# Hybrid decoder step: key steps ahead of the attention units, the block chain spread over them, query tiles upwards, value steps in the last eight units

## The chip, the core and the metric

One Trainium2 chip, one of its cores. The metric is the device time of one launch in microseconds (us), the median of several runs. The core has five engines that run their own instruction streams and meet at semaphores: PE (TensorE, matrix products into eight PSUM banks), DVE (VectorE), ACT (ScalarE), POOL (GpSimd) and SP (SyncE). SP, ACT and POOL start DMAs; sixteen DMA engines carry them.

## What is computed

One inference step of a one-layer decoder, for a prompt of 512 tokens and for 8 samples of 8 new tokens with 2048 past tokens each, all in float32. Cut to what matters:

```python
q, kv_cmp, kv_slc, kv_win, gates, u = in_projection(x, ...)           # one product with w_in
kc, vc = compress_blocks(kv_cmp, cmp_pos_emb, w_cmp_k, w_cmp_v, ...)  # 64 tokens of a block -> 1 key, 1 value
#   kc = einsum('bnlkd,lde->bnke', blk[..., 0], w_cmp_k), then RMSNorm;  vc likewise, without the norm
o_cmp, p_kv = compressed_attention(q, q_pos, kc, vc, slopes)
idx, valid  = select_blocks(p_kv, q_pos, nb)                          # top 16 blocks of 64 tokens
o_slc = selected_branch(q, q_pos, kv_slc, idx, valid, slopes)
o_win = window_attention(q, q_pos, kv_win, k_pos, slopes)             # last 512 tokens
A = gates0 * o_cmp + gates1 * o_slc + gates2 * o_win
h = x + concat(A, pool_mix(u)) @ w_out
y = h + hier_moe(rmsnorm(h))                                          # 16 experts, 2 for each token
```

For the samples the past tokens of the compressed and of the selected branch lie in pages of 128 tokens in HBM and are found through a page table: 16 pages for each of 8 samples.

## The kernel before, in words

The kernel is one hand-ordered program. Each engine has one block of code, and the order in it is the order of its instructions; a semaphore for each PSUM bank says that it is filled or read (`opened`, `filled`, `written`, `read`, `taken`), and `psum_plan` walks the same loops to give every named product its bank. In order of time:

1. Input projection (to about 127 us), PE at work all the time.
2. Pooling mixer in four groups, then the transposes of the queries and keys of five row tiles.
3. Prompt attention, here called **the units**. A unit u is one entry of `prompt_pairs()`: query tile i (128 queries), head pair g, branch b (selected or window). There are 32. Tile i attends to i + 1 blocks of 128 keys, so a unit of tile 3 costs four times the columns of a unit of tile 0. `AHEAD` = 3: in the pass of unit u of the loop PE makes the scores of unit u + 3 (L1047), then transposes the exponentials of unit u (L1091), and in every second unit multiplies with the values (L1060). DVE turns the scores into logits (L1886) and copies one half of the transposes back (L1938), ACT takes the exponentials (L1506) and copies the other half (L1535). PE's transposes of unit u + 1 need DVE's and ACT's copies of unit u. After four units the shares are multiplied in (L1071, L1906 to L1912).
4. Sample attention in four pairs of samples (`s_scores`, `s_values`), first line L1113.
5. Output projection, router, and the experts (from about 490 us), where PE is at work nearly all the time.

**Block compression** runs beside stages 2 and 3 in two rounds of HD = 64 steps: round 0 for keys, round 1 for values. A step d is four small products on PE (L914, eight records in a trace) and needs chunk d of the cached rows, regrouped for it. POOL regroups all chunks of round 0 (L2319); in round 1 POOL does every second, DVE (L1945) and ACT (L1556) every fourth. The chunks lie in a ring of `RING` = 13: chunk d may be written when step d - 13 is done. The key steps are spread: `AT_HEAD` before the mixer, `AT_MIX` in each of its groups, `AT_TURN` behind each row tile's transposes, the rest in the units of `CMP_UNITS`; the value steps are all in units.

The cached rows come in pages of 64 KB: samples 0 to 3 by SP (L692), samples 4 to 7 by POOL (L2298), each with a `DMA` per page and a read of 16 page numbers into registers per sample. The value pages overwrite the key pages, so both engines wait until the last key chunk is regrouped. When the last value chunk is regrouped, the same memory takes the pages of the selected branch: SP loads samples 0 and 2 (L752) and POOL, which waits for the end of the last value step, samples 1 and 3 (L2306). The first product of stage 4 needs all pages of samples 0 and 1.

**The chain**: with the compressed keys done, the kernel computes their norm, the block logits of the samples (`cmp_s`) and of the prompt (`pc_s`), the probabilities, their sum over heads, the top 16 blocks (the mask) and, with the compressed values, the transposes `vcT` and `pc_T`. Each of these is done by `beside(u)` of each engine in a unit with a number of its own, `AT_NORM` = 3 to `AT_TURNED` = 26:

```python
AT_NORM, AT_KEYS, AT_LOGITS, AT_PROBS, AT_SUM, AT_MASK, AT_VALUES, AT_TURNED = \
    3, 4, 6, 7, 9, 10, 25, 26
```

The same number holds for all engines: in unit 6, for instance, PE makes both sets of block logits (L988, L995), DVE waits for them, works on them and lets ACT take the exponentials. On DVE these steps stand between the logits of unit u + 3 and the copy of unit u.

## Time and profile before

| | us |
|---|---|
| median of 3 runs | 778.77 (777.96 to 780.96) |
| the profiled execution, its own time | 777.04 |
| its span | 775.3 |
| PE busy | 731.8 (94%) |
| DVE, POOL, ACT busy | 268.1, 232.1, 171.1 |
| mean granted PE clock | 0.969 |

The profile is of one execution. The span runs from its first to its last instruction; 1.7 us lie around it. PE has the largest share, but the share is an average over the stages: the page's digits show stretches in which PE is below nine tenths and its clock below full speed, and they lie between 180 and 390 us. A granted clock of 1.00 is 2.4 GHz and one of 0.50 is 1.2 GHz.

### The profile page before, as it was taken

The numbers are of one execution on the slowest core, as the hardware profiler recorded it, in microseconds if no ns is written. First come the engines' busy times: TensorE is split into PE (matmuls) and PEld (weight loads), VectorE is DVE, ScalarE is ACT, GpSimd is POOL, SyncE is SP. The second block draws the span as 40 slices with busy tenths as digits, with TensorE's granted clock in tenths as the row PEclk, the third lists the DMA queues.
The fourth block names the chain that finished last, engine by engine and source line by source line (L and its number), as shares of the span: only waits on it lengthen the run. The fifth ranks groups of instructions, "written<-read, shape, count | busy, mean of one in ns | idle before, by whom it ended". The sixth has DMA issues, their size and how long they took to land.

```text
span 775.3 us, 16562 instructions
## 1 busy us (share of the span) xinstructions
PE 731.8 (94%) x6460; PEld 409.2 (53%) x6460; DVE 268.1 (35%) x722; ACT 171.1 (22%) x367; POOL 232.1 (30%) x393
## 2 busy tenths in 40 slices
PE   6999999997899978888999999999999999999998
PEld 3555456755656745566745555344555544455542
DVE  1200062248568656766413238101111101011147
ACT  3100030335347543423210010110111001101000
POOL 2464276644668456566200001000000000000050
PEclk9999999979889977999999999999999999999999
DMA  9956541316751099777799036388999999999974
GB/s 288 257 156 217 161 106 36 91 33 164 192 162 31 17 294 323 256 209 216 211 350 394 28 147 243 128 322 327 399 411 420 429 415 421 421 417 421 387 254 144
DMA packets 81937, 191.78 MB, mean 247 GB/s; under 512 B 15798, under 2 KB 54982, under 8 KB 77373
## 3 DMA queue, kind: packets, MB, share of 16 engines
q1 hardware_dynamic: 67461, 150.63, 54.2%
q0 software_dynamic: 12160, 31.97, 12.8%
q10 hardware_dynamic: 2240, 8.13, 2.6%
q8 instruction: 52, 0.85, 0.4%
q14 instruction: 24, 0.20, 0.1%
HBM read 174.09 MB, written 16.70 MB: 246 GB/s over the span
## 4 chain that ended last, share of the span: by engine, by line
PE 82%; DVE 9%; issue 3%; DMA 3%; ACT 1%; SPq 1%; POOL 0%; DVEq 0%; POOLq 0%
PE bank L1339 31%; PE bank L897 13%; PE bank L1240 7%; PE bank L914 5%; PE bank L1047 3%; PE bank L1060 3%; PE bank L1091 2%; PE bank L894 2%; PE bank L1323 2%; DVE arena L1981 1%; PE bank L1186 1%; PE bank L1431 1%; PE bank L1269 1%; PE bank L1113 1%; PE bank L1231 1%
## 5 line engine op out<-in xcount | busy, mean ns | idle before, releaser
L1339 PE MATMUL bank<-arena,proj 128*32 128x256 f32 (+1 forms) x2352 | 238.7, 483 | 1.3 <-DVE proj L2199 0.8
L1339 PEld LDWEIGHTS bank<-arena,proj 128*32 128x32 f32 x2352 | 103.6, 110 | 96.1 <-issue 77.6
L897 PE MATMUL bank<-arena,amT 128*128 128x454 f32 x256 | 102.5, 559 | 1.1 <-DMA arena<-in_w_in 1.1
L2385 POOL DMA_INDIRECT proj<-normed_rows,idx x12 | 11.4, 952 | 301.5 <-PE bank L1323 193.9
L2298 POOL DMA_DIRECT2D arena<-in_cache_cmp_kv x128 | 68.8, 537 | 64.3 <-issue 55.3
L2209 DVE TENSOR_TENSOR proj<-proj,bank 128x256 f32<-128x256 f32 x24 | 10.0, 420 | 209.8 <-PE bank L1339 209.8
L897 PEld LDWEIGHTS bank<-arena,amT 128*128 128x128 f32 x256 | 48.9, 194 | 50.0 <-issue 49.6
L2306 POOL DMA_DIRECT2D arena<-in_cache_slc_kv x96 | 51.6, 537 | 41.0 <-issue 34.5
L1339 PE MATMUL bank<-amT,proj 128*32 128x512 f32 (+1 forms) x336 | 56.5, 532 | 0.0
L1339 PE MATMUL bank<-queries_and_bias,proj 128*32 128x512 f32 (+1 forms) x384 | 56.5, 486 | 0.0
L2319 POOL COPY arena<-arena 128x268 f32<-128x268 f32 x64 | 38.2, 653 | 39.3 <-PE bank L914 22.1
L1506 ACT ACTIVATE arena<-arena,st 128x512 f32<-128x512 f32 (+3 forms) x48 | 26.6, 555 | 51.0 <-DVE st L1886 51.0
L1633 ACT ACTIVATE proj<-bank 128x512 f32<-128x512 f32 x24 | 14.4, 598 | 82.1 <-PE bank L1339 82.1
L1339 PEld LDWEIGHTS bank<-queries_and_bias,proj 128*32 128x32 f32 x384 | 21.4, 110 | 17.3 <-issue 13.7
L1091 PE MATMUL bank<-mats,arena 128*128 128x128 f32 x120 | 20.4, 301 | 10.6 <-ACT proj L1535 6.0
L1886 DVE CUSTOM_DVE_ANT_0 arena<-bank,queries_and_bias 128x512 f32<-128x512 f32 (+3 forms) x48 | 21.8, 488 | 23.1 <-PE bank L1047 23.0
L1339 PEld LDWEIGHTS bank<-amT,proj 128*32 128x32 f32 x336 | 19.4, 110 | 19.1 <-issue 17.4
L1240 PE MATMUL bank<-arena,amT 128*128 128x512 f32 x64 | 29.0, 597 | 0.0
L1619 ACT ACTIVATE proj<-bank 128x512 f32<-128x512 f32 x12 | 7.2, 597 | 98.5 <-PE bank L1323 98.5
L1060 PE MATMUL bank<-proj 128*64 128x256 f32 x160 | 25.6, 459 | 0.5 <-DVE proj L1938 0.5
L2396 POOL DMA_INDIRECT arena<-expert_rows,row_i x8 | 7.9, 985 | 57.0 <-DMA expert_rows<-proj 54.8
L1626 ACT ACTIVATE proj<-bank 128x512 f32<-128x512 f32 x12 | 7.2, 598 | 79.1 <-PE bank L1339 79.1
(358 smaller groups left out, 1031.1 us busy)
## 6 DMA issues: line engine op xcount, KB each, us to landing
arena<-in_w_up SPq DMA_DIRECT2D x13, 2048.0 KB, 16.6
arena<-in_w_down SPq DMA_DIRECT2D x13, 2048.0 KB, 16.7
arena<-in_w_gate SPq DMA_DIRECT2D x10, 2048.0 KB, 17.0
arena<-in_cache_cmp_kv POOLq DMA_DIRECT2D x128, 64.0 KB, 2.3
arena<-in_cache_cmp_kv SPq DMA_DIRECT2D x128, 64.0 KB, 2.2
amT<-in_w_gate SPq DMA_DIRECT2D x3, 2048.0 KB, 13.0
queries_and_bias<-in_w_gate SPq DMA_DIRECT2D x3, 2048.0 KB, 11.8
expert_rows<-proj ACTq DMA_DIRECT2D x11, 512.0 KB, 9.6
```

What stands on the lines that cost most here:

```text
L897: last = pe.matmul(ps(("in", c, i))[0:n, 0:WC], xnT[:, k, i * P:i * P + n], w_in[c % 2][:, k, :], start=k == 0, stop=k == KC - 1)
L914: last = pe.matmul(ps(("cmp", r, par))[64 * g:64 * g + 64, 0:2 * SIDE], w_cmp[r][rows, d, :], chunks[r][d % RING][rows, g, :], start=d == ...
L1047: written(pe.matmul(ps(("p_s", u, k))[:, 0:n], qT[rows, g, i * P:(i + 1) * P], kt[rows, 0:n], start=True, stop=True), ("p_s", u, k))
L1060: last = pe.matmul(ps(("p_o", v // 2))[64 * k:64 * k + 64, g * P:(g + 2) * P], proj[:, c, v0 + 64 * k:v0 + 64 * k + 64], pT[v % 2][:, c, k ...
L1091: last = pe.transpose(ps(("p_T", u, k))[:, c * P:(c + 1) * P], pS[u % 4][:, k, c * P:(c + 1) * P], ident)
L1240: last = pe.matmul(ps(("h", i, half))[0:n, :], amT[:, k, i * P:i * P + n], out_matrix(k, half), start=k == 0, stop=k == KC - 1)
L1339: ins = pe.matmul(dst[part, :], rows[:, part], own if q < TRIO else shared, start=start, stop=stop)
L1506: sc.activation(z, z, ACT.Exp, bias=st[:, m:m + 1], scale=-1.0, accum_out=st[:, d:d + 1]).then_inc(p_e, 1)
L1886: read(ve.tensor_tensor_reduce(pS[u % 4][:, k, 0:n], ps(("p_s", u, k))[:, 0:n], dist[:, SEQ - n:SEQ], -SLOPES[g + G * k], 3e38, ALU.add, A ...
L2298: po.dma_start(sides[:, 1, (b - 4) * PAGES + k, :], src).then_inc(ld_last, 16)
L2306: po.dma_start(pages[b % 4][:, k, first * P:(first + count) * P], src)\
L2319: po.tensor_copy(chunk_out(r, d), chunk_in(d)).then_inc(regrouped, 1)
```

## The change

- `prompt_pairs` takes the query tiles upwards (0, 1, 2, 3) instead of downwards.
- `AT_HEAD` is 13 instead of 8, `AT_TURN` 2 instead of 3. `DONE` stays 8 + 16 + 15 = 13 + 16 + 10 = 39.
- The remaining 25 key steps leave units 0 and 1 and stand ahead of the unit loop, in three parts behind the scores of units 0, 1 and 2. DVE takes the compressed keys in unit 0 (before: unit 2).
- The 64 value steps go from units 15 to 22 to units 23 to 30.
- Each step of the chain has a unit of its own on each engine, and each consumer stands at least one unit behind its producer.
- SP loads the first 8 of the 16 value pages of sample 4, which POOL loaded before.

```diff
-CMP_UNITS = [(0, 2), (15, 8)]
+VALUE_UNITS = 23, 8
-AT_HEAD, AT_MIX, AT_TURN = 8, 4, 3
+AT_HEAD, AT_MIX, AT_TURN = 13, 4, 2
...
-    return [(i, 2 * gp + e, b) for i in (3, 2, 1, 0) for b in range(2) for gp in range(2) for e in range(2)]
+    return [(i, 2 * gp + e, b) for i in (0, 1, 2, 3) for b in range(2) for gp in range(2) for e in range(2)]
...
+def compress_fill():
+
+    return [(0, d) for d in range(DONE, HD)]
...
-AT_NORM, AT_KEYS, AT_LOGITS, AT_PROBS, AT_SUM, AT_MASK, AT_VALUES, AT_TURNED = \
-    3, 4, 6, 7, 9, 10, 25, 26
+    first, count = VALUE_UNITS
+    return share([(1, d) for d in range(HD)], count, u - first) if first <= u < first + count else []
+
+
+PE_KEY_MEAN, PE_LOGITS, PE_PC, PE_SUM, PE_VALUES, PE_TURNED = 2, 9, 10, 15, 32, 34
+DVE_MEAN, DVE_KEYS, DVE_LOGITS, DVE_PROBS, DVE_SCORE, DVE_PC, DVE_PC_PROBS, DVE_MASK, DVE_CLEAR = 3, 6, 10, 13, 16, 17, 19, 20, 34
+ACT_ROOT, ACT_EXP, ACT_PC_EXP, ACT_VALUES, ACT_TURNED = 5, 12, 18, 33, 34
...
             load_wcmp(1)
             load_cache(1, 1, 3)
+            sp.load(regs, table_rows[4:5, :])
+            for k in range(PAGES // 2):
+                page = sp.snap(regs[k], min_val=0, max_val=a["cache_cmp_kv"].shape[0] - 1)
+                src = a["cache_cmp_kv"][bass.ds(page, 1), :, 1:2, :, :].rearrange("a p c h d -> (a p) (c h d)")
+                sp.dma_start(sides[:, 1, k, :], src).then_inc(ld_cache, 16)
...
-                    opened(pe, "pc_s")
-                    for i in range(4):
-                        for j in range(G):
-                            c = i * H * NBP + j * 2 * NBP
-                            last = pe.matmul(ps("pc_s")[:, c:c + 2 * NBP], qT[:, j, i * P:(i + 1) * P], kpb[:, :], start=True, stop=True)
-                    written(last, "pc_s")
...
+                if PE_PC <= u < PE_PC + 4:
+
+                    i = u - PE_PC
...
             for u in range(AHEAD):
                 p_scores(u)
+                for r, d in share(compress_fill(), AHEAD, u):
+                    compress(r, d)
...
-                for k in range(PAGES):
+                for k in range(PAGES // 2 if kv and b == 4 else 0, PAGES):
...
-            po.wait_ge(ld_cache, 2 * 64 * 16)
-            po.wait_ge(ld_last, 2 * 64 * 16)
+            po.wait_ge(ld_cache, (2 * 64 + 8) * 16)
+            po.wait_ge(ld_last, (2 * 64 - 8) * 16)
```

On PE, from the last row tile's transposes into the first units (key steps are L914 with `xh` as the second name, scores L1047, transposes L1091). Before:

```order
L914 MATMUL bank<-arena,xh 64x134 x12
L970 MATMUL bank<-gate,amT 128x24 x4
L1047 MATMUL bank<-kTs,queries_and_bias 128x512 x8
L914 MATMUL bank<-arena,xh 64x134 x16
L1091 MATMUL bank<-mats,arena 128x128 x8
L914 MATMUL bank<-arena,xh 64x134 x32
L1047 MATMUL bank<-kTw,queries_and_bias 128x512 x2
L914 MATMUL bank<-arena,xh 64x134 x16
L1091 MATMUL bank<-mats,arena 128x128 x8
L914 MATMUL bank<-arena,xh 64x134 x36
```

The same place of the changed kernel (its L922, L978, L1059 and L1105 are L914, L970, L1047 and L1091 of before):

```order
L922 MATMUL bank<-arena,xh 64x134 x8
L978 MATMUL bank<-gate,amT 128x24 x4
L1059 MATMUL bank<-kTs,queries_and_bias 128x128 x2
L922 MATMUL bank<-arena,xh 64x134 x32
L1059 MATMUL bank<-kTs,queries_and_bias 128x128 x2
L922 MATMUL bank<-arena,xh 64x134 x32
L1059 MATMUL bank<-kTs,queries_and_bias 128x128 x2
L922 MATMUL bank<-arena,xh 64x134 x36
L1059 MATMUL bank<-kTs,queries_and_bias 128x128 x2
L1105 MATMUL bank<-mats,arena 128x128 x2
```

The 25 key steps (100 products) now stand between the first three scores, which have 128 columns instead of 512.

On PE, from the last value steps on (value steps are L914 with `arena` as the second name; L1007 is `vcT`, L1113 the first line of the sample attention). Before, with 18 more rows ahead of L1113:

```order
L914 MATMUL bank<-xh,arena 64x134 x12
L1047 MATMUL bank<-kTs,queries_and_bias 128x128 x2
L1091 MATMUL bank<-mats,queries_and_bias 128x128 x4
L1047 MATMUL bank<-kTs,queries_and_bias 128x128 x2
L1091 MATMUL bank<-mats,arena 128x128 x2
L1060 MATMUL bank<-proj 64x256 x4
L1047 MATMUL bank<-kTw,queries_and_bias 128x128 x2
L1007 MATMUL bank<-mats,xh 128x128 x2
```

The changed kernel (L1019 is `vcT`, L1027 `pc_T`, L1072 and L1083 the values and shares, L1127 the first line of the sample attention):

```order
L922 MATMUL bank<-xh,arena 64x134 x12
L1105 MATMUL bank<-mats,queries_and_bias 128x128 x8
L1019 MATMUL bank<-mats,xh 128x128 x2
L1019 MATMUL bank<-mats,xh 8x128
L1072 MATMUL bank<-proj 64x256 x8
L1027 MATMUL bank<-mats,proj 64x128 x4
L1083 MATMUL bank<-mats,shares 128x128 x4
L1127 MATMUL bank<-mats,arena 128x128 x16
```

Between the last value step and the sample attention there were eleven and a half units; now there is the rest of one.

## Rows read from the trace of the kernel before

**Rows 1.** Busy time by stretch: from:to, length, each engine's busy, PEclk, DMA share, GB/s

```profile
177.00:222.00 45.00, 38.02 (x236) 24.38 (x228) 29.37 (x105) 19.10 (x46) 25.80 (x48) 0.85 0.72 188
222.00:237.00 15.00, 13.13 (x91) 8.01 (x90) 13.64 (x59) 10.10 (x31) 9.20 (x17) 1.00 0.49 141
237.00:270.60 33.60, 33.60 (x630) 23.41 (x626) 22.85 (x64) 22.35 (x60) 22.69 (x32) 1.00 0.02 6
270.60:294.50 23.90, 17.33 (x88) 10.16 (x89) 11.46 (x55) 10.96 (x42) 13.47 (x26) 0.73 0.91 289
```

**Rows 2.** Timeline of PE, marks of the stage: start, length, instructions [idle before]

```profile
155.71 0.96 PE L970 MATMUL bank<-gate,amT 64*128 64x24 f32 x7
...
170.09 2.06 PE L914 MATMUL bank<-arena,xh 64*64 64x134 f32 x64
...
197.13 4.47 PE L995 MATMUL bank<-kpb,queries_and_bias 128*128 128x16 f32 x32
...
238.09 0.69 PE L914 MATMUL bank<-xh,arena 64*64 64x134 f32 x16
...
269.66 0.92 PE L914 MATMUL bank<-xh,arena 64*64 64x134 f32 x24
...
294.49 3.62 PE L1113 MATMUL bank<-mats,arena 128*128 128x128 f32 x16
```

**Rows 3.** Timeline of PE: work of one unit, and scores that mark the pace

```profile
177.45 1.13 PE L1047 MATMUL bank<-kTw,queries_and_bias 64*128 64x512 f32 x4
178.51 1.09 PE L1091 MATMUL bank<-mats,arena 128*128 128x128 f32 x8
179.53 1.95 PE L1060 MATMUL bank<-proj 128*64 128x256 f32 x16
...
221.35 1.07 PE L1047 MATMUL bank<-kTw,queries_and_bias 64*128 64x384 f32 x4
...
232.70 0.93 PE L1047 MATMUL bank<-kTs,queries_and_bias 64*128 64x256 f32 x4
...
278.02 0.80 PE L1047 MATMUL bank<-kTw,queries_and_bias 64*128 64x128 f32 x4
...
284.69 0.69 PE L1047 MATMUL bank<-kTw,queries_and_bias 64*128 64x128 f32 x4 [0.77 <-DVE st L1886]
```

**Rows 4.** Timelines of DVE and ACT: steps of the chain

```profile
177.55 0.16 DVE L1749 COPY posc<-bank 128x1 f32<-128x1 f32 x1 [1.52 <-PE bank L914]
...
179.53 0.43 DVE L1924 TENSOR_TENSOR xh<-xh 128x264 f32<-128x264 f32 x1
...
184.48 1.86 DVE L1793 COPY QB<-qTs 64x32 f32<-64x32 f32 x16
...
188.31 1.80 DVE L1808 RECIPROCAL xh<-xh 128x264 f32<-128x264 f32 x1
...
192.46 0.17 DVE L1816 MEMSET xh<- 128x132 f32 x1
```

```profile
184.95 1.28 ACT L1516 ACT_TABLE_LOAD   x1
```

**Rows 5.** Timeline of POOL: regroupings (L2319), prompt values (L2324), page DMAs (L2306)

```profile
170.64 4.82 POOL L2319 COPY arena<-arena 128x268 f32<-128x268 f32 x8 [0.40 <-PE bank L914]
...
236.36 0.62 POOL L2324 COPY arena<-proj 128x512 f32<-128x512 f32 x1 [3.00 <-DMA arena<-in_cache_cmp_kv]
...
275.08 2.38 POOL L2306 DMA_DIRECT2D arena<-in_cache_slc_kv  x4 [10.80 <-issue]
277.83 7.28 POOL L2306 DMA_DIRECT2D arena<-in_cache_slc_kv  x12 [0.37 <-issue]
```

**Rows 6.** Timeline of SP's queue, value pages: start, length, DMAs

```profile
178.54 8.62 SPq L692 DMA_DIRECT2D arena<-in_cache_cmp_kv  x16
...
195.56 39.38 SPq L692 DMA_DIRECT2D arena<-in_cache_cmp_kv  x48
```

**Rows 7.** The page's DMA issues: size, median us from issue to landing

```profile
arena<-in_cache_slc_kv POOLq DMA_DIRECT2D x32, 128.0 KB, 5.2
```

More of the change, by code:

```diff
@@ L144, in compress_turn @@
     return [(0, d) for d in range(DONE - AT_TURN * (TILES - i), DONE - AT_TURN * (TILES - i - 1))]
+def compress_fill():
+    return [(0, d) for d in range(DONE, HD)]
 def compress_steps(u):
-    for r, (first, count) in enumerate(CMP_UNITS):
-        if first <= u < first + count:
-            done = DONE if r == 0 else 0
-            return share([(r, d) for d in range(done, HD)], count, u - first)
-    return []
-AT_NORM, AT_KEYS, AT_LOGITS, AT_PROBS, AT_SUM, AT_MASK, AT_VALUES, AT_TURNED = \
-    3, 4, 6, 7, 9, 10, 25, 26
+    first, count = VALUE_UNITS
[3 more added lines that the diff above has]
+ACT_ROOT, ACT_EXP, ACT_PC_EXP, ACT_VALUES, ACT_TURNED = 5, 12, 18, 33, 34
 def psum_plan():
@@ L201, in psum_plan @@
                 add(("cmp", 1, 1), bank=5)
[L202 to L203 removed]
+        for at, names in ((PE_KEY_MEAN, [("key_norm", 5)]), (PE_LOGITS, [("cmp_s", 4)]), (PE_PC, [("pc_s", 5)]), (PE_SUM, [("cmp_sum", 4)]),
+                          (PE_VALUES, [("vcT", 5)]), (PE_TURNED, [("pc_T", 5)])):
             if u == at:
```

67 lines of the change are left out of this document (39 added, 28 removed).

## The prediction

> **What bounds the kernel now.** I read the busy times by stretch first, because the change touches one stage only, the units between about 156 and 294 us. What comes ahead of it (the projection) and behind it (sample attention, output projection, experts) keeps its order and can only move as a whole. So the question is when the sample attention starts: at 294.49 before [rows 2].
>
> The stretches tell three kinds of time apart [rows 1]. From 237.0 to 270.6 PE is busy for all 33.6 us at full clock: these are the value steps between units of tiles 2 and 1. From 222 to 237 DVE is busy for 13.64 of 15 us, so DVE sets the pace. From 177 to 222 and from 270.6 to 294.5 nobody is full: PE has 38.0 of 45 and 17.3 of 23.9 us, at a mean clock of 0.85 and 0.73. That is where the engines wait for each other, in the chain of steps between 177 and 222 and in the thin units behind the value steps. In that last stretch, though, the DMA engines are busy for 0.91 of the time: they bring the pages that the sample attention needs. This cover matters more than the waits.
>
> Marks of before [rows 2]: scores begin at 156.6 (behind L970), the first value step is at 238.1, the last ends at 269.66 + 0.92 = 270.6, the sample attention starts at 294.5.
>
> **Head and turns.** Five steps go to the head and five leave the turns. PE is never idle there, a step costs the same in both places (8 steps in 2.06 us, 0.26 each [rows 2]), so the sum is 0, and the turns still end at 156.6. POOL's ring is refilled at 0.60 us a chunk (8 in 4.82 [rows 5]) and by then has its 13 chunks.
>
> **Key steps ahead of the units.** PE has 3 scores of 0.4 us and 25 × 0.26 = 6.5, together 7.7 us. The ring holds chunks to 51, and the other 12 cost POOL 12 × 0.60 = 7.2 us from 157.3 on: the last at 164.6, the last step at about **165.0**. Before, the last key chunk was ready at 170.64 + 4.82 = 175.5 [rows 5].
>
> **Units 0 to 22.** I take a pace for each tile and add what a chain step costs over the slack of its engine. A chain step on DVE delays the copy of its unit, and with it PE's next transposes; PE can do only one score ahead.
> - Unit 0: DVE takes the compressed keys in 2.4 us (177.55 to 179.96 [rows 4]), then a logit and a copy: 3.3 us, to 168.3.
> - Tile 0: three units from 278.02 to 284.69 [rows 3], 2.2 us each with two transposes of the chain among them; I take 2.0 for each of units 1 to 7, 14.0. In the last stretch of [rows 1] eight such units lie; DVE's 11.46 us less 3.3 for the value chain are 1.0 each, ACT's 10.96 are 1.4. Unit 3 adds 0.43 + 1.86 on DVE [rows 4], of which 1.4 show. Unit 5 adds two table loads of 1.28 [rows 4] and a root of 0.42 on ACT: 2.4 show. Unit 6 adds 188.31 to 192.63 = 4.3 on DVE [rows 4]: 3.4 show. In total 7.2. In the kernel before these three stood beside units of tile 3, whose PE work is 1.06 + 1.02 + 0.95 = 3.0 us [rows 3], and hid behind it for the most part. At 189.5.
> - Tile 1: the value stretch gives 32.5 us for 8 units and 64 steps [rows 2]; less 64 × 0.26 = 16.7 that is 2.0 a unit, all PE. I take 2.05, 16.4 for units 8 to 15. The prompt's block logits cost 4.47 us for 32 records, partly at the lower clock [rows 2]; spread over four units 2.2 to 4.4, of which with the samples' logits and DVE's part 3.2 show. At 209.1 so far, at full clock.
> - The clock in these thin units: in the last stretch it was 0.73, from 222 to 237 it was 1.00 [rows 1]. At 1.2 GHz a unit of tile 1 is 3.7 us on PE. At 0.85 (177 to 222) 30% of the time is at the lower clock, a mean of 2.4 a unit, +2.5; at 0.73 it is 2.7, +5.2; at 1.00 nothing. I take 3.5, since these units follow thin ones. At 212.6.
> - Tile 2, units 16 to 22: from 221.35 to 232.70 there are four such units with a mask step, 2.84 each [rows 3]. Four without a mask at 2.65 and three with it at 2.85 make 19.2; the prompt's logits and probabilities on DVE (1.7 and 2.3 us) show with 2.2, the first scores of tile 3 with 0.5. 21.9, unit 23 begins at **234.5**, its value steps behind one score at 235.6.
>
> **Value pages.** They can start when the last key chunk is regrouped, 164.6 instead of 175.5. SP began 3.1 us behind it, at 178.54, and its last issue ended at 195.56 + 39.38 = 234.94 [rows 6], 56.4 us for 64 pages. It now has 72: 16 more register reads and 8 issues of 0.54, about 8 us. 164.6 + 3.1 + 56.4 + 8 = 232.1, and as before POOL's next copy 1.4 us behind, its 0.6 and one chunk of 0.6 [rows 5]: the first chunk at about **234.7**. POOL, with 56 pages, is done earlier and waits for SP. The pages are then just hidden, with 1 us to spare: if the units were faster, the pages would be the limit.
>
> **Value steps.** Before 32.5 us with, among them, 5 scores of tile 1 and 2 of tile 0, the transposes and values of tile 1: 14.4 us. Now 5 scores of tile 3 (5.3), transposes (7.9), values (7.1), shares (1.1): 21.4. DVE, ACT and POOL had 22.9, 22.4 and 22.7 of the 33.6 us [rows 1]; the wider units give DVE and ACT some 7 us more, in 39.5, so PE remains the limit. 32.5 + 7.0 = 39.5: the last value step ends at **275.1**, 4.5 us later than before.
>
> **What was hidden and is not now.** POOL loads the selected pages of sample 1 only behind the last value step: first DMA 4.5 us behind it (270.6 to 275.08), last issue at 285.11 [rows 5], landing 5.2 us later [rows 7]: 290.3, **19.7 us behind the last value step**. Before, eleven units took 23.9 us and covered it. Now the rest of the units is a transpose, DVE's value chain of some 3 us, one product and two transposes, some 8 us, and PE then waits some 12 us. The sample attention starts at 275.1 + 19.7 = 294.8. It starts behind a long wait; before it began at the lower clock too, so I add only 1.0 for a longer lower stretch: 295.8, against 294.5. The second pair needs samples 2 and 3, whose pages landed some 33 us behind the last value step, and starts 34 us behind it: no wait, but no reserve.
>
> **The sum**: the value steps start 2.5 us earlier (235.6 for 238.1), last 7.0 longer, the sample attention follows 4.2 closer behind them (19.7 for 23.9), and its start costs 1.0: +1.3 us, 777.04 + 1.3 = 778.3 for the profiled execution. Its own time is 1.7 us under the median of 778.77, so I forecast 778.77 + 1.3 = **780.0**.
>
> **Rivals.**
> - *The thin units stay at the lower clock (slower).* The mechanism is tiles 0 and 1 first, with PE work of 1.1 and 1.9 us a unit and waits of 2 to 3.5 us at units 0, 3, 5 and 6. For it: 0.73 in the only stretch of such units [rows 1]. Against it: the key steps ahead run dense, and 222 to 237 has 1.00 in spite of waits. If all of tiles 0 and 1 ran at 1.2 GHz, it would be 7 × 0.4 + 8 × 1.65 - 3.5 = +12.5; half of that, +6, is the likelier size: 786. It decides once unit 23 begins 2.6 us later than 234.5. The Trainium skill (TensorE: Matmul & The Clock Gate, "HAM oscillation — how this bites in real kernels") describes bursts of products with waits between them that fall back to the lower clock again and again; by that rule the time is the upper end, 792. The trace agrees with it in part: the thin stretch fell back, but not for all of its time. Chance 0.26.
> - *The pages take longer (slower).* The 19.7 us rest on one landing figure and on one pace; a read of page numbers took 3 to 4.5 us where it can be seen [rows 5, 6], and SP's gap of 8.4 us between its two rows [rows 6] holds another. Both queues together may cost 5 us more, and the second pair then waits too: 785. Chance 0.10.
> - *The pages come sooner and the units keep up (faster).* SP's 72 issues at 0.54 with reads of 3 us would be done by 223, and without any chain cost the units need only until 215. If both go halfway, the value steps start at 226 and end at 265.5, the sample attention starts at 286: -9, 770. For it: the spread does take the waits of PE for DVE out of the chain. Against it: DVE's and ACT's work in the chain remains, beside less PE work. The Trainium skill (DMA: Bandwidth & Descriptors, "Issuing engines are not separate DMA queues") says that issuing from several engines saves only issue time. By that rule the eight moved pages cost nothing and the first chunk is there at 226 instead of 234.7. The trace speaks partly against it, since the DMA share from 177 to 222 is 0.72 and not 1. Chance 0.13.
> - *It changes nothing that shows*, my forecast: 0.51.
>
> **How the numbers follow.** This kernel's measurement tells about 0.5% (3.9 us) from no change. Forecast 780.0 within 774.9 to 782.7: 0.51; slower 0.36 from two rivals; faster 0.13. Unknown bounds: landing between 1.4 us (the compressed pages [rows 5]) and twice 5.2 (-4, +5), units to 23 between 215 and 247 (below 234 hidden by the pages, above it +12), restart 0 to 2. The range 771 to 791 leaves out the far ends of both sides, 0.2.
>
> **What the profile after would show.** The last key step at about 165; unit 23 at 232 to 237; POOL's L2324-like copy at about 233 with a wait for SP's pages; value steps from 235 to 275 with PE full at clock 1.00; a wait of PE of about 12 us ahead of the sample attention, released by the selected pages of POOL's queue; the last 480 us unchanged in length. I am wrong if unit 23 comes before 230 or after 240, if PE does not wait ahead of the sample attention, or if the pages land less than 15 us behind the last value step.

## The result, and the profile after

| | before | changed |
|---|---|---|
| median | 779.87 us (777.96 to 783.20, 4 runs: the three known before and one more) | 790.82 us (787.87 to 793.44, 4 runs) |
| profiled execution | 777.04 us | 793.44 us |
| mean granted clock of it | 0.969 | 0.957 |

The ratio is 1.0123 (95% interval 1.0080 to 1.0165): slower by 6 to 13 us. The profiled execution is the slowest of its four, and some 9 us of it lie at its end: one block of 128 products of the last experts (L1353) takes 16.0 us there (754.8 to 770.8), with short waits of PE and a clock of 0.79, against 7.1 us in the trace of e2 below. Of the other traces of this study only e12's shows the same (14.3 us). So I compare the traces up to the **projection start** (the first product of the output projection, L1240 before, L1254 in the changed kernel): 387.73 before and 397.58 now, +9.85 us.

The stretches of the changed kernel, cut at its own marks (columns as in [rows 1]):

```profile
164.20:188.80 24.60, 17.96 (x67) 9.13 (x67) 16.14 (x81) 11.86 (x41) 13.21 (x25) 0.56 0.70 169
188.80:217.40 28.60, 28.28 (x150) 19.03 (x150) 14.35 (x56) 13.63 (x46) 16.92 (x32) 0.72 0.62 181
217.40:242.40 25.00, 21.97 (x128) 11.67 (x127) 20.80 (x77) 17.08 (x47) 4.82 (x8) 1.00 0.18 51
242.40:282.30 39.90, 39.54 (x665) 27.17 (x663) 25.30 (x63) 23.24 (x50) 17.30 (x25) 1.00 0.04 9
282.30:301.30 19.00, 7.53 (x44) 4.69 (x40) 5.50 (x18) 3.43 (x7) 9.52 (x18) 0.71 0.86 277
301.30:397.60 96.30, 83.98 (x733) 58.05 (x733) 58.63 (x148) 30.14 (x53) 52.66 (x95) 0.95 0.82 249
```

The first row is units 0 to 7 (tile 0): PE works 18 of 24.6 us, at a clock of 0.56. The second is tile 1: PE is full, for 28.3 of 28.6 us, and the clock is 0.72. A dense stretch at a low clock is not new, though. Ahead of the stretches of [rows 1], the kernel before has PE full for 9.0 us at 0.50, in the scores of units 1 to 3, behind a wait of 0.94 us, and once more for 5.9 us at 0.50 (199.9 to 205.8):

```profile
158.66 8.41 PE L1047 MATMUL bank<-kTs,queries_and_bias 64*128 64x512 f32 x12 [0.94 <-DVE st L1886]
```

```profile
159.30:168.30 9.00, 9.00 (x36) 3.77 (x38) 4.20 (x12) 5.39 (x15) 0.48 (x1) 0.50 0.00 0
```

So the remark ahead of the prediction that such stretches lie between 180 and 390 us leaves one out. With the key steps between the scores it is gone: the changed kernel has 1.00 from 156 to 165. What is new is the length: from 167.0 to 204.6 the clock is at or near 0.50, and for the last 15.6 us of that PE is full. The fourth row is the value steps, PE full at 1.00; the fifth the wait for the selected pages. PE's timeline: the wait in unit 0, the scores with which PE's passes of units 8, 16 and 23 begin, the samples' block logits, first and last value steps, sample attention, projection (L1059 is L1047 of before):

```profile
167.02 0.98 PE L1059 MATMUL bank<-kTw,queries_and_bias 64*128 64x128 f32 x4 [2.03 <-DVE st L1907]
188.80 1.56 PE L1059 MATMUL bank<-kTs,queries_and_bias 64*128 64x256 f32 x4 [0.87 <-DVE st L1907]
193.55 3.62 PE L996 MATMUL bank<-KCT,QB 128*128 128x32 f32 x16
217.43 1.36 PE L1059 MATMUL bank<-kTs,queries_and_bias 64*128 64x384 f32 x4
241.34 1.13 PE L1059 MATMUL bank<-kTs,queries_and_bias 64*128 64x512 f32 x4
242.40 0.46 PE L922 MATMUL bank<-xh,arena 64*64 64x134 f32 x8
281.41 0.92 PE L922 MATMUL bank<-xh,arena 64*64 64x134 f32 x24
293.93 1.12 PE L1127 MATMUL bank<-mats,arena 128*128 128x128 f32 x4 [2.56 <-DMA arena<-in_cache_slc_kv]
301.25 2.82 PE L1127 MATMUL bank<-mats,arena 128*128 128x128 f32 x12 [6.21 <-DMA arena<-in_cache_slc_kv]
304.00 1.98 PE L1136 MATMUL bank<-arena,QB 128*64 128x512 f32 x4
```

```profile
397.58 3.70 PE L1254 MATMUL bank<-arena,amT 128*128 128x512 f32 x8
```

POOL's timeline answers [rows 5]:

```profile
232.80 0.62 POOL L2345 COPY arena<-proj 128x512 f32<-128x512 f32 x1 [18.61 <-DMA arena<-in_cache_cmp_kv]
286.47 7.28 POOL L2327 DMA_DIRECT2D arena<-in_cache_slc_kv  x12 [11.32 <-PE bank L1019]
```

### The profile page after: what moved, and what is told of

It is laid out like the page before. It is cut to its first block, busy times and chain, and to the rows that moved or that the text cites. A ratio compares the mean times of both kernels' runs of the same rounds, so it can differ in the third digit from the quotient of the medians.

```text
span 791.7 us, 16565 instructions
## 1 busy us (share of the span) xinstructions
PE 739.5 (93%) x6460; PEld 411.6 (52%) x6460; DVE 265.8 (34%) x722; ACT 170.9 (22%) x367; POOL 226.8 (29%) x385
## 4 chain that ended last, share of the span: by engine, by line
PE 78%; SPq 8%; DVE 5%; issue 4%; DMA 2%; ACT 1%; POOL 1%; DVEq 0%; ACTq 0%
PE bank L1353 33%; PE bank L905 13%; PE bank L1254 7%; SPq L760 3%; PE bank L922 3%; SPq L756 3%; PE bank L1059 3%; PE bank L1072 2%; PE bank L1105 2%; PE bank L902 2%; PE bank L1337 2%; PE bank L1445 1%; PE bank L1283 1%; PE bank L1200 1%; POOL arena L2340 1%
## 5 line engine op out<-in xcount | busy, mean ns | idle before, releaser
L1353 PE MATMUL bank<-arena,proj 128*32 128x256 f32 (+1 forms) x2352 | 244.8, 487 | 3.9 <-issue 2.5
L1353 PEld LDWEIGHTS bank<-arena,proj 128*32 128x32 f32 x2352 | 105.7, 111 | 102.8 <-issue 85.6
L2319 POOL DMA_DIRECT2D arena<-in_cache_cmp_kv x120 | 64.5, 538 | 60.5 <-issue 52.2
L1353 PE MATMUL bank<-amT,proj 128*32 128x512 f32 (+1 forms) x336 | 56.5, 532 | 0.0
L1353 PE MATMUL bank<-queries_and_bias,proj 128*32 128x512 f32 (+1 forms) x384 | 56.5, 486 | 0.0
L1520 ACT ACTIVATE arena<-arena,st 128x128 f32<-128x128 f32 (+3 forms) x48 | 26.6, 554 | 39.3 <-DVE st L1907 39.3
L1648 ACT ACTIVATE proj<-bank 128x512 f32<-128x512 f32 x24 | 14.3, 598 | 87.1 <-PE bank L1353 87.1
L1353 PEld LDWEIGHTS bank<-queries_and_bias,proj 128*32 128x32 f32 x384 | 21.4, 110 | 17.3 <-issue 13.7
L1907 DVE CUSTOM_DVE_ANT_0 arena<-bank,queries_and_bias 128x128 f32<-128x128 f32 (+3 forms) x48 | 21.7, 488 | 23.0 <-PE bank L1059 22.6
L1353 PEld LDWEIGHTS bank<-amT,proj 128*32 128x32 f32 x336 | 19.3, 110 | 19.1 <-issue 17.4
L1254 PE MATMUL bank<-arena,amT 128*128 128x512 f32 x64 | 29.0, 596 | 0.1
L1634 ACT ACTIVATE proj<-bank 128x512 f32<-128x512 f32 x12 | 7.2, 597 | 96.8 <-PE bank L1337 96.8
L1105 PE MATMUL bank<-mats,arena 128*128 128x128 f32 x120 | 21.4, 309 | 6.6 <-ACT proj L1550 3.7
L1127 PE MATMUL bank<-mats,arena 128*128 128x128 f32 x128 | 19.2, 304 | 8.8 <-DMA arena<-in_cache_slc_kv 8.8
L2340 POOL COPY xh<-arena 128x268 f32<-128x268 f32 x32 | 21.5, 701 | 20.2 <-PE bank L922 20.2
L1072 PE MATMUL bank<-proj 128*64 128x256 f32 x160 | 25.1, 450 | 0.3 <-DVE proj L1959 0.3
```

Source lines behind the costliest of these rows:

```text
L1072: last = pe.matmul(ps(("p_o", v // 2))[64 * k:64 * k + 64, g * P:(g + 2) * P], proj[:, c, v0 + 64 * k:v0 + 64 * k + 64], pT[v % 2][:, c, k ...
L1105: last = pe.transpose(ps(("p_T", u, k))[:, c * P:(c + 1) * P], pS[u % 4][:, k, c * P:(c + 1) * P], ident)
L1254: last = pe.matmul(ps(("h", i, half))[0:n, :], amT[:, k, i * P:i * P + n], out_matrix(k, half), start=k == 0, stop=k == KC - 1)
L1353: ins = pe.matmul(dst[part, :], rows[:, part], own if q < TRIO else shared, start=start, stop=stop)
L1520: sc.activation(z, z, ACT.Exp, bias=st[:, m:m + 1], scale=-1.0, accum_out=st[:, d:d + 1]).then_inc(p_e, 1)
L2319: po.dma_start(sides[:, 1, (b - 4) * PAGES + k, :], src).then_inc(ld_last, 16)
```

## Experiments

Each run has its ratio to the kernel before, timed on the same chip at the same time; medians of different sessions are not compared. One table holds the marks of all traces: the last value step's end, the first score products of the sample attention (L1122 before, L1136 in the changed kernel), the projection start, and its distance to both.

| kernel | value end | first products | projection | behind value end | behind products | time ratio (95%) |
|---|---|---|---|---|---|---|
| before | 270.6 | 298.0 | 387.7 | 117.2 | 89.7 | 1 |
| changed | 282.3 | 304.0 | 397.6 | 115.3 | 93.6 | 1.0123 (1.0080 to 1.0165) |
| e1_down | 273.8 | 295.8 | 390.3 | 116.5 | 94.5 | 1.0024 (0.9995 to 1.0054) |
| e2_values_20 | 278.3 | 299.7 | 395.9 | 117.6 | 96.2 | 1.0081 (1.0047 to 1.0116) |
| e3_dense | 284.5 | 306.5 | 397.9 | 113.3 | 91.3 | 1.0104 (1.0042 to 1.0166) |
| e4_before_up | 271.4 | 307.3 | 397.2 | 125.9 | 89.9 | 1.0111 (1.0082 to 1.0139) |
| e5_down_v20 | 272.6 | 294.6 | 393.4 | 120.8 | 98.7 | 1.0044 (1.0018 to 1.0071) |
| e6_down_v18_pages | 266.6 | 289.7 | 380.9 | 114.3 | 91.2 | 0.9975 (0.9949 to 1.0001) |
| e7_dense_more | 276.9 | 298.4 | 390.9 | 114.0 | 92.5 | 1.0096 (1.0059 to 1.0134) |
| e8_before_fill | 267.4 | 292.3 | 384.1 | 116.7 | 91.8 | 0.9968 (0.9942 to 0.9994) |
| e9_fill_v13 | 263.4 | 293.3 | 382.7 | 119.3 | 89.5 | 0.9992 (0.9965 to 1.0020) |
| e10_compact | 262.4 | 284.2 | 375.5 | 113.2 | 91.3 | 0.9950 (0.9922 to 0.9978) |
| e11_read_ahead | 282.6 | 301.8 | 396.3 | 113.7 | 94.5 | 1.0101 (1.0063 to 1.0138) |
| e12_compact_read | 265.5 | 287.0 | 378.4 | 112.9 | 91.4 | 0.9901 (0.9865 to 0.9937) |

The marks are those of one execution each, taken on several chips, and executions of one kernel differ: before took 768.8 to 778.9 us in 25 runs on one chip. e10's trace is its fastest run (763.4, median 769.6) and e5's its slowest (783.1, median 777.3). e12's edit to e10 touches nothing ahead of the value steps, yet its value steps start 3.1 us later. So a difference of 1 to 3 us between two marks shows little by itself; the ratios carry more.

### The tile order, undone and alone

**e1_down** undoes it in the changed kernel, **e4_before_up** does it alone in the kernel before:

```diff
-    return [(i, 2 * gp + e, b) for i in (0, 1, 2, 3) for b in range(2) ...
+    return [(i, 2 * gp + e, b) for i in (3, 2, 1, 0) for b in range(2) ...
```

> The changed kernel with one part undone: the query tiles are taken downwards (3, 2, 1, 0) as before. Key steps ahead, chain spread and value steps in units 23 to 30 stay. Theory A (the loss comes from the tile order: thin units of tiles 0 and 1 at the lower clock, and tile 3's wide units in the value stretch): units 0 to 7 need 3.9 us each of PE and hide the chain, unit 23 begins at about 236 us instead of 241.3, the value stretch is short (64 steps of 0.26 and thin units, about 30 us instead of 39.9) and ends at 266 instead of 282.3, the sample attention starts 19 us behind it, at about 285 instead of 304; time about 770, below both kernels. Theory B (the loss comes from the page wait of the sample attention alone, which this order keeps in full): the wait stays and the time is 786 or more. Theory C (the chain spread or the key steps ahead cost by themselves): unit 23 comes at 241 or later here too.

> The kernel before with one part of the change done alone: the query tiles are taken upwards. Key steps, chain and value steps (units 15 to 22) stay in their units. Theory A (the order is the cause): thin units behind the key steps run at the lower clock, unit 15 is reached at about 215, PE waits there for the value pages until about 238, the value steps take some 33 us to 271 and the eight units of tile 3 behind them 4.1 us each: the sample attention starts at 302 to 306, time 786 to 792. Theory B (the order costs nothing without the late value steps): within 3 us of the kernel before, 776 to 782.

Undone, the loss falls from 1.2% to 0.2%. Alone, the order costs 1.1%. So it is the order that made the kernel slower, and the other parts of the change together show no gain (the interval of 1.0024 holds 1). The parts of theory A held only in part: e1's clock was near full (0.93 to 1.00 from 165 to 240) and its value stretch 28.4 us instead of 39.9, but the pass of unit 23 began at 245.0 and not at 236, the value steps, though their pages had been there since 234, with it, and the time is not below that of before. Theory C's mark, unit 23 at 241 or later in this order too, came true: 23 units with the spread chain take long in either order. So part of the late value steps is not the order's.

In e4_before_up the cost has another face. PE's pass of unit 15 begins at 223.2, and PE stands before the value pages; then eight wide units follow the value steps, and the sample attention starts with no page wait, but late:

```profile
231.98 1.17 PE L914 MATMUL bank<-xh,arena 64*64 64x134 f32 x16 [7.87 <-POOL xh L2319]
304.88 1.91 PE L1113 MATMUL bank<-mats,arena 128*128 128x128 f32 x16
```

### The clock: products that nobody reads

**e3_dense** (44 added products) and **e7_dense_more** (58) fill PE's waits in units 0 to 8; their output goes to a bank that is free there and is not used:

```diff
+EXTRA = {0: 8, 1: 3, 2: 3, 3: 8, 4: 3, 5: 8, 6: 8, 7: 3}    # e7_dense_more: 7: 11, 8: 6
...
                 beside(u)
+                if u in EXTRA:
+                    if u == 0:
+                        taken(pe, "gate_rows")
+                    for _ in range(EXTRA[u]):
+                        pe.matmul(bank[4][:, 0:P], ident, ident, start=True, stop=True)
```

> The changed kernel with products added that nobody reads, into a bank that is free there: 8 of 128x128 in units 0, 3, 5 and 6, 3 in units 1, 2, 4 and 7, 44 in all, 11.9 us at 0.27 us each, each set ahead of the unit's transposes, where PE waits for DVE and ACT. Theory A (the clock falls because PE waits there, and the lower clock then stretches the units of tile 1): the granted clock is 1.00 from 165 to 215 instead of 0.55 and 0.70, unit 16 comes at about 213 instead of 217.4 and the time is 3 to 5 us under the changed kernel's, 786 to 788. Theory B (DVE and ACT set the pace of these units, and the clock is a mark and not a cause): the clock rises and unit 16 stays at 217 or comes later by the added work; time 790 to 796.

> The changed kernel with unread products in units 0 to 8: as in the run with 44 of them, but 11 instead of 3 in unit 7 and 6 in unit 8, 58 in all. With 44 the granted clock stood at 1.00 to 189 us and fell behind two waits of 1.27 and 1.01 in unit 7; units 0 to 8 came at the same times at either clock, and units 9 to 13 then ran at 0.50 as in the changed kernel. Theory A (the clock in tile 1 is what costs): the clock stays at 1.00 through 215, the block logits of the samples take 1.97 instead of 3.62 us, unit 16 comes 4 to 6 us earlier than with 44 (212 to 214 instead of 218.1) and the output projection 3 to 5 us earlier; time 0.3% to 0.6% under the run with 44. Theory B (DVE and ACT set the pace in tile 1 too): the clock stays high and unit 16 comes at 217 or later.

With 44 products the clock stays at 1.00 until 189 and then falls, behind two waits of unit 7. The two rows of those waits and the block logits of the samples, then the stretches (e3_dense):

```profile
187.41 0.30 PE L1111 MATMUL bank<-mats,queries_and_bias 128*128 128x128 f32 x1 [1.27 <-DVE proj L1965]
188.73 1.55 PE L1060 MATMUL bank<-kTs,queries_and_bias 64*128 64x256 f32 x4 [1.01 <-DVE st L1913]
...
193.46 3.62 PE L997 MATMUL bank<-KCT,QB 128*128 128x32 f32 x16
```

```profile
165.90:189.00 23.10, 20.62 (x159) 16.15 (x156) 16.33 (x83) 12.17 (x41) 12.88 (x24) 1.00 0.67 164
189.00:204.60 15.60, 15.60 (x66) 10.71 (x65) 6.27 (x25) 6.28 (x22) 9.63 (x18) 0.50 0.75 216
```

Tile 1 then runs as in the changed kernel, and the theory's gain of 3 to 5 us did not come: the clock rose in tile 0 only, where it is worth 2 us. With 14 more, in units 7 and 8, it holds through tile 1 (e7_dense_more, timeline, then stretches):

```profile
188.32 1.04 PE L1060 MATMUL bank<-kTs,queries_and_bias 64*128 64x256 f32 x4 [0.61 <-DVE st L1913]
...
192.48 1.97 PE L997 MATMUL bank<-KCT,QB 128*128 128x32 f32 x16
...
211.10 1.36 PE L1060 MATMUL bank<-kTs,queries_and_bias 64*128 64x384 f32 x4
```

```profile
165.60:188.30 22.70, 21.91 (x174) 17.60 (x170) 15.94 (x81) 11.88 (x40) 12.89 (x24) 1.00 0.68 164
188.30:211.10 22.80, 22.46 (x162) 15.56 (x163) 14.18 (x56) 13.61 (x46) 13.35 (x25) 1.00 0.72 203
211.10:235.00 23.90, 20.87 (x124) 11.36 (x123) 19.81 (x76) 15.93 (x45) 3.81 (x9) 1.00 0.34 95
```

The same products take 1.97 instead of 3.62 us, tile 1 takes 22.8 instead of 28.6, and unit 16 comes at 211.1. Counted from the last scores ahead of the units (164.13 in the changed kernel, 165.6 here) unit 16 is 7.8 us earlier: 5.8 of it in tile 1, 2.0 in tile 0. The cost in tile 1 can be up to 1.6 us more, since six of the added products stand in unit 8, where PE was busy without a gap (L1104, 1.60 us from 189.29 on). Theory A's marks came true (unit 16 at 211.1, the projection 6.9 us earlier than with 44 products), and its time did not: 0.3% to 0.6% were expected, and 1.0096 against 1.0104 and 1.0123 are within each other's intervals. So in the trace the low clock costs the changed kernel some 8 us up to unit 16. One piece of the difference can be seen: in e7's trace the projection now waits 2.02 us for its weights, the clock falls there, and eight of its products take 6.43 instead of 3.70 us. Another: the value pages come at 235.0 in this trace and PE waits 0.47 us for the first chunk, so the value steps start only 5.8 us earlier than in the changed kernel. With the clock at 1.00 through tiles 0 and 1 the kernel is still 1.0% slower than before, while the order undone leaves 0.2%. By the times, then, the clock of these units is not shown to be the larger part of what the order costs; what the rest is stays open.

### Where the value steps stand

**e2_values_20** moves them three units forward in the changed kernel (`VALUE_UNITS = 20, 8`). **e5_down_v20** does that with the tiles downwards.

> The changed kernel with the value steps three units earlier: units 20 to 27 instead of 23 to 30, all else as in the changed kernel. Theory A (clock of the thin units is the larger part, +4.8 us up to unit 16, and is untouched here; the uncovered loading of the selected pages is the smaller part): the value steps start at about 235 instead of 242.4, since their first chunk is there at 234, and end at about 272; the pages land 19 us later, at 291, and units 28 to 31 with 4.1 us each cover them; the sample attention starts at 294 to 297 instead of 304: time 781 to 784. Theory B (PE's work ahead of the sample attention sets its start and the page wait is only its other face): the start stays within 2 us of 304 and the time at 788 to 791.

> The changed kernel with two parts changed: tiles downwards and value steps in units 20 to 27. In the traces so far the output projection starts either 113 to 118 us behind the last value step or 90 us behind the first score products of the sample attention, whichever is later. Theory D (the last value step anchors the page loads of all four pairs of samples, so its time counts and not only the first wait): value steps start at 235, when their pages are there, instead of 245.4, and end at 266 instead of 273.8; the output projection starts at 381 to 384 (before: 387.7, downward order alone: 390.3), time 0.4% to 0.8% under the kernel before. Theory E (PE's own work and the waits of thin units set the start, as the sum in the prediction had it): with the same work on PE nothing moves against the downward order alone, time 0% to 0.4% above the kernel before.

e2 did half of what was expected of it: the value steps start at 235.4 as expected, but end at 278.3 instead of 272; the first score products come at 299.7, 4.3 us earlier, where some 7 to 10 had been expected; the ratio is 0.4% lower, within the intervals. The projection is only 1.7 us earlier. Between them lie waits that the kernel before doesn't have:

```profile
298.18 1.53 PE L1127 MATMUL bank<-mats,arena 128*128 128x128 f32 x12 [1.60 <-DMA arena<-in_cache_slc_kv]
...
311.82 1.97 PE L1127 MATMUL bank<-mats,arena 128*128 128x128 f32 x16 [1.76 <-DMA arena<-in_cache_slc_kv]
...
349.94 1.06 PE L1150 MATMUL bank<-mats,xh 128*128 128x128 f32 x4 [3.63 <-DMA xh<-in_state_win_kv]
```

The changed kernel has the last of them too, in its third pair of samples:

```profile
352.18 0.66 PE L1150 MATMUL bank<-mats,xh 128*128 128x128 f32 x4 [0.84 <-DMA xh<-in_state_win_kv]
353.67 0.66 PE L1150 MATMUL bank<-mats,xh 128*128 128x128 f32 x4 [0.83 <-DMA xh<-in_state_win_kv]
```

And the chain that ended last goes through SP's queue there, from the selected pages to the window states (changed kernel, start, us, what):

```profile
330.56 4.25 SPq L756
334.92 2.56 SPq L756
338.78 1.09 SPq L760
347.94 5.69 DMA xh<-in_state_win_kv
```

This gave theory D: the last value step frees the memory, and from there the loads of all eight samples queue up. In the table the projection starts never sooner than 112.9 us behind the value end and never sooner than 89.5 behind the first products. Before, e4 and e9 sit on the second limit, with 4 to 13 us of slack on the first; the changed kernel, e3, e6, e7, e10, e11 and e12 sit within 2.5 us of the first. e1, e2, e5 and e8 are off both, by 2 to 8 us; the first three have waits for pages or window states and a clock below 1.00 in their second and third pairs. So these are the least of fourteen values and not a formula, and theory D is an argument from them: e11 and e12 below test it.

e5 went against the theory in its size. Its value steps started at 237.1 and ended at 272.6, not 266, and the projection came at 393.4, not at 381 to 384: in the downward order units 20 to 23 carry the masks on DVE, PE waited 3.09 us for a chunk that DVE regroups (240.61), the clock fell (0.83 from 235 to 255), and the second pair waited 3.26 for its pages. Moving the value steps into the masks gained nothing: 1.0044, just above theory E's 0% to 0.4%.

### The key steps, the pages and a closer chain

**e8_before_fill** does the key steps' part alone in the kernel before; **e9_fill_v13** adds value steps in units 13 to 20:

```diff
-CMP_UNITS = [(0, 2), (15, 8)]
+CMP_UNITS = [(0, 0), (15, 8)]      # e9_fill_v13: (13, 8)
-AT_HEAD, AT_MIX, AT_TURN = 8, 4, 3
+AT_HEAD, AT_MIX, AT_TURN = 13, 4, 2
...
                 p_scores(u)
+                for r, d in share(compress_fill(), AHEAD, u):
+                    compress(r, d)
```

> The kernel before with one part of the change done alone: 13 key steps in the head, 2 behind each row tile, and the other 25 ahead of the units. Tiles downwards, the chain's units and the value steps' units (15 to 22) as before. The key chunks are regrouped at 164 instead of 175.5 and the value pages can start 11 us earlier. Theory D (the value pages held the value steps: POOL waited 3.0 us for them ahead of 238.1): the first chunk is there at about 227, the value steps start when unit 15 does, at 233 to 236 instead of 238.1, and end at 266 to 268; the output projection 2 to 4 us earlier, time 0.2% to 0.5% under the kernel before. Theory E (key steps ahead of the units only move work and lengthen the wait of the chain): the time is within 0.1% of the kernel before or above it.

> The kernel before with the key steps ahead of the units (as in the run with that part alone) and the value steps in units 13 to 20 instead of 15 to 22. With the key steps ahead POOL had the value pages at 226.2 and waited, and the value steps began at 234.9 with unit 15. Theory D (the last value step anchors the rest): value steps begin at 228 to 229 and end at 261 to 263 instead of 267.4, the output projection starts at 377 to 380 instead of 384.1; time 0.8% to 1.2% under the kernel before. Theory E (the units' own work sets the sample attention's start): the value steps move and the sample attention's first score products stay within 1 us of 292.3; time 0.2% to 0.4% under the kernel before, as without the move.

e8: POOL's copy ahead of the first value chunk stands at 226.2 instead of 236.4, value steps run from 234.9 to 267.4, the projection starts at 384.1, the ratio is 0.9968: the marks and the time that theory D gave. Its reason, that the value pages held the value steps, is not shown: before, PE goes from its score at 237.46 to the first value step at 238.09 without a wait. What brings unit 15 forward, from 237.5 to 234.2, can be seen in the first scores. Before, those of units 1 to 3 take 8.4 us behind a wait; in e8 key steps stand between them and each takes 1.13 us at a clock of 1.00:

```profile
159.31 1.13 PE L1052 MATMUL bank<-kTs,queries_and_bias 64*128 64x512 f32 x4
```

Three of them are 3.4 us, so 5.0 us less; 3.2 are left at unit 15. Without the earlier pages (POOL's copy stood at 236.4) PE would have had to wait there, so both are needed; no run separates them. e9: the value steps moved (228.1 to 263.4) and the first products did not (293.3); the projection kept 89.5 us behind them. Here theory E was right, since the units' own work is the limit once the value steps are early. The ratio, 0.9992, shows no gain over before, where theory E gave 0.2% to 0.4% and theory D 0.8% to 1.2%.

**e6_down_v18_pages** has the tiles downwards, `VALUE_UNITS = 18, 8`, and gives POOL its eight pages back. **e10_compact** draws the chain together:

```diff
-PE_KEY_MEAN, PE_LOGITS, PE_PC, PE_SUM, PE_VALUES, PE_TURNED = 2, 9, 10, 15, 32, 34
+PE_KEY_MEAN, PE_LOGITS, PE_PC, PE_SUM, PE_VALUES, PE_TURNED = 2, 9, 10, 13, 27, 28
-DVE_MEAN, ..., DVE_MASK, DVE_CLEAR = 3, 6, 10, 13, 16, 17, 19, 20, 34
+DVE_MEAN, ..., DVE_MASK, DVE_CLEAR = 3, 6, 10, 12, 14, 14, 16, 17, 29
-ACT_ROOT, ACT_EXP, ACT_PC_EXP, ACT_VALUES, ACT_TURNED = 5, 12, 18, 33, 34
+ACT_ROOT, ACT_EXP, ACT_PC_EXP, ACT_VALUES, ACT_TURNED = 5, 11, 15, 28, 29
```

> As the kernel with downward tiles, but the value steps go to units 18 to 25 and POOL loads the eight value pages of sample 4 itself again (64 pages on each queue instead of 72 and 56). Theory D (the last value step is the anchor): SP ends its issues at 227 instead of 232.7, the first chunk is there at 229, value steps run from 229 to 261, the output projection starts at 376 to 380; time 0.9% to 1.4% under the kernel before. Theory E: the units set the pace, the value steps only move within them; time as with the downward order alone, 0% to 0.4% above the kernel before. If moving the eight pages back makes POOL the late queue, the value steps start at 233 or later and the time is that of units 20 to 27.

> The kernel with downward tiles, value steps in units 18 to 25 and 64 pages on each queue, with the second half of the chain closer together: sum over heads in unit 13 instead of 15, the prompt's logits and probabilities on DVE in units 14 and 16 instead of 17 and 19, the masks in units 17 to 20 instead of 20 to 23, the transposes behind the value steps in units 27 and 28 instead of 32 and 34. Theory D: DVE's waits in the value stretch (1.72 and 1.38 us of PE) shrink, the value steps end at 262 to 264 instead of 266.6, and with the transposes no longer behind the last unit PE is ready before the pages; the output projection starts at 376 to 379 instead of 380.9; time 0.5% to 0.9% under the kernel before. Rival (the added DVE work in units 14 to 17 costs there what it saves later): the value steps start later than 231, time 0.1% to 0.4% under the kernel before.

e6: first copy at 227.9 (232.8 in the changed kernel), so 64 pages for each queue is the better balance. The key steps stand ahead in all of these traces: with 72 and 56 pages the copy stands at 232.8 to 235.4 in either tile order, with 64 and 64 at 225.3 to 227.9. e6's other marks: value steps 230.7 to 266.6 (expected 261), with two waits of PE for DVE of 1.72 and 1.38; projection at 380.9 (expected 376 to 380); ratio 0.9975 with 1 in its interval. The expected 0.9% to 1.4% did not come. e10 took those waits down to one of 0.70; its value steps end at 262.4, as expected, and the transposes no longer stand behind the last unit:

```profile
281.06 3.24 PE L1122 MATMUL bank<-mats,arena 128*128 128x128 f32 x16
...
375.54 5.40 PE L1249 MATMUL bank<-arena,amT 128*128 128x512 f32 x8 [1.13 <-DMA arena<-in_w_out]
```

No wait for pages stands ahead of the sample attention, and the ratio is 0.9950 (0.9922 to 0.9978): below both kernels.

### The page numbers read ahead

**e11_read_ahead** (in the changed kernel) and **e12_compact_read** (in e10):

```diff
+            po.load(page_regs, a["page_table"][1:2, :])
             for par in range(2):
                 filled(po, ("cmp", 1, par))
             slc_pages(1, 0, 2)            # and the same on SP for sample 0
```

The read inside `slc_pages` and `load_slc` is left out for these two samples.

> The changed kernel with one thing moved: the 16 page numbers of sample 1 (POOL) and of sample 0 (SP) are read into registers ahead of the waits for the end of the value steps instead of behind them. In the changed kernel POOL's first page DMA came 4.1 us behind the last value step and SP's 2.8 us behind the last regrouped chunk. Theory D (queues and their reads hold the pages, and PE waits for the pages): both start about 3 us earlier, the long wait ahead of the sample attention ends about 3.5 us earlier (16 us behind the last value step instead of 18.9), and the output projection starts at least 2 us earlier; time 0.3% to 0.5% under the changed kernel, so 0.7% to 1.0% above the kernel before. Rival (the DMA engines are full and the bytes set the landing): the DMAs start earlier and land at the same time; no change in the time.

> The kernel with the closer chain (downward tiles, value steps in units 18 to 25, 64 pages on each queue) and, added, the page numbers of samples 0 and 1 read ahead of the waits. In the closer chain PE was ready before the pages no longer: the sample attention began without a wait, and later waits were small (0.29 us for pages, 1.04 for window states, 1.13 for the output weights). Theory D (the output projection starts no sooner than 113 us behind the last value step, because the loads of all samples queue up from there): the loads start 3 us sooner, these later waits shrink, and the projection starts 1 to 3 us sooner, at 110 to 112 us behind the last value step; time 0.6% to 0.9% under the kernel before. Rival (PE's own 90 us from the first score products of the sample attention are the limit by now): the projection stays at 90 to 91 us behind them, time 0.5% under the kernel before, unchanged.

e11's rows, POOL and PE:

```profile
283.40 7.28 POOL L2330 DMA_DIRECT2D arena<-in_cache_slc_kv  x12 [8.00 <-PE bank L924]
```

```profile
299.02 2.82 PE L1129 MATMUL bank<-mats,arena 128*128 128x128 f32 x12 [6.48 <-DMA arena<-in_cache_slc_kv]
```

POOL's first DMA comes 0.8 us behind the last value step instead of 4.1, and the wait ends 16.4 us behind it instead of 18.9: of the 3.3 us that the reads took behind the release, 2.5 reach the landing, so the rival, that the bytes alone set it, is wrong. The projection starts at 396.3, 1.3 us sooner than in the changed kernel (2.1 counted from the start of the units, which came 0.8 later), 113.7 behind the value end; expected were 2 or more and a ratio of 1.007 to 1.010. e12 hardly shortened the distance: POOL's first page DMA comes 0.8 us behind the value end instead of e10's 4.0, and the projection 112.9 instead of 113.2. That speaks against theory D in its strict form, in which the start of the loads sets this distance: the first products came 21.5 us behind the value end (21.9 in e10), the projection again 91.4 behind them, with 2.00 us of waiting for its weights. By the trace the rival was right, with 91 us of the sample attention as the limit. By the time neither was: 0.6% to 0.9% and 0.5% under before were expected. Its ratio, 0.9901 (0.9865 to 0.9937), is the best of the study, but it was taken on another chip than e10's; how much of the step from 0.9950 the reads gave stays open.

## Why the prediction was right or wrong

The time, 790.82, lies just inside the range of 771 to 791, the forecast of 780.0 missed it by 10.8, and "within 0.5%" was wrong: it was slower. That it lies inside is luck in part: the range had room for a late unit 23 (up to 247) and none for the sample attention, which took 3.9 us more, and it holds by 0.2 us. By its own test the first rival happened, which had a chance of 0.26: unit 23 had to begin 2.6 us behind 234.5, and it began 6.8 behind it. But the agreement with its upper size, 792, is luck too. The lower clock costs 7.8 us by e7, 4.3 more than the forecast had for it and less than the rival's likelier +6; the rest of the loss is work that the forecast had too short, and the sample attention.

Step by step:
- **Head, turns, key steps**: turns end at 155.4 (156.6 forecast), the last key step at 164.2 (165.0). Right.
- **Tile 0**: unit 8 at 188.8 against 189.5. Right in the sum, for a reason that was not in it: 2.0 of the 24.7 us are the clock.
- **Tile 1**: 28.6 us against 23.1. Two terms were short. The clock was put at 3.5 and is 5.8 (28.6 less e7's 22.8). The block logits of samples and prompt were let show with 3.2 us; in e7 they are 1.97 and four times 1.06, 6.2 us of PE, and PE is busy for 22.46 of the 22.8, so they show in full. 19.6 without the clock should have been about 22.8. Since 1.6 us of e7's 22.8 are added products, the split can shift by that much: 5.8 to 7.4 for the clock, 22.8 to 21.2 for the rest.
- **Tile 2**: 23.9 against 21.9, in the changed kernel and in e7 alike. In e7 PE has 20.9 and DVE 19.8 of it: neither is full, and they wait for each other's steps. Short by 2.0.
- **Value pages**: POOL's copy at 232.8, as forecast, but PE was ready for it only at 242.4. The pages were not the limit, and the eight moved pages made them late by 5 us or more (232.8 to 235.4 in seven traces with them, 225.3 to 227.9 in five without). So the third rival's argument, by which the moved pages cost nothing, does not hold here.
- **Value steps**: 39.9 us against 39.5. Right; e1 shows 28.4 for the same steps beside thin units.
- **Selected pages**: 18.9 us behind the last value step against 19.7, PE waits 8.8 against 12. Right for the landing. e11 adds what the distance is made of: 3.3 us of it are reads of page numbers behind the wait.
- **"The last 480 us unchanged in length"**: wrong by 3.9 us (93.6 against 89.7 from the first products to the projection). The sum treated the sample attention as a block that starts when the first two samples are there. "No wait, but no reserve" was said of the second pair alone; it is true of the third, where PE waits 0.84 and 0.83 us for window states, whose loads stand behind the pages in SP's queue. The clock is the rest of what can be seen: 0.96 from the first products to the projection instead of 1.00, with PE busy for 81.3 us instead of 78.4. Behind the projection start the profiled execution is 6.5 us longer than before, which is its block of late experts; what that is in the other runs is not known.

The sum again: -0.7 (unit 8), +5.5, +2.0, +0.4 make the value end 7.2 us later than forecast. From there the first products follow 2.6 us sooner than forecast (0.8 of the landing, and 4 of the 16 transposes done within the wait), which leaves 4.6. With 1.3 forecast that is 5.9 of the 6.0 seen; and 3.9 in the sample attention make the 9.85.

The Trainium skill (TensorE: Matmul & The Clock Gate, "HAM oscillation — how this bites in real kernels") names the mechanism: short bursts of products with waits between them fall back to the lower clock. The forecast took it for a rival because 222 to 237 had stood at 1.00 in spite of waits [rows 1]. The trace agrees with the page for tile 0, where the clock fell behind a wait of 2.03 us in unit 0. But tile 1 has hardly a wait (28.28 of 28.6 us busy) and still had 0.72: here the dense stretch paid for the thin one ahead of it.

## What to carry to other kernels

When thin work and dense work may be put in either order, look at what runs right behind the thin work: in these traces the dense stretch behind short waits ran at 0.50 for 6 to 16 us, and most of what the clock cost was paid there (5.8 of 7.8 us). When the end of one stage frees the memory of the next, follow the loads behind the first that is waited for too: in the changed kernel the third pair still waited for its own. And change one part at a time: here the tile order alone cost 1.1%, the key steps alone gave 0.3%, and together they read as "the change is slower". A trace is one execution: a mark that moves by 2 us is not yet a gain in the median.

## What the runs showed of the hardware that I had not expected

- With PE full, the granted clock can stay at 0.50 for 15.6 us (e3_dense, 189.0 to 204.6, PE busy 15.60 of 15.60).
- 58 products that nobody reads, 15.7 us of PE time at 0.27 each, made units 0 to 15 shorter by 7.8 us, since most of them stood in waits: the clock was 1.00 from 165.6 to 235.0.
- Reading 16 page numbers into registers costs 3.3 us ahead of the first DMA on POOL (4.1 us behind the release with the read, 0.8 without).
- Behind a single wait of 0.94 us PE was full for 9.0 us at 0.50 in the kernel before (159.3 to 168.3).
